# Down weights of 32 experts in two loads of 2 MB, with up-product columns dealt by four

## Chip, cores and metric

The kernel runs on one core of one Trainium2 chip. The metric is the device time of an execution in microseconds. Before the change it is 1321.36 us in the median of three runs (1321.18 to 1321.95).

## What is computed

One inference step of a hybrid decoder layer on 256 prompt tokens and 8 sequences of 8 sample tokens (320 tokens of width 1024), in float32: a modulated norm, an input projection, retention and mLSTM heads, an output projection, then a router that picks 4 of 32 experts for each token, and the final norm. What bears on the change is the experts:

```python
def expert(args):
    xe, e = args
    hu = xe @ w_up[e] + b_up[e]                       # [slots, 1024] @ [1024, 2048]
    gate = jnp.minimum(hu[:, :D_FF], SWIGLU_LIMIT)
    lin = jnp.clip(hu[:, D_FF:], -SWIGLU_LIMIT, SWIGLU_LIMIT)
    glu = gate * jax.nn.sigmoid(SWIGLU_ALPHA * gate)
    return ((lin + 1.0) * glu) @ w_down[e] + b_down[e]  # [slots, 1024] @ [1024, 1024]
```

An expert's up weights are 8 MB, its down weights 4 MB; all 32 experts are loaded, some 400 MB.

## The kernel before, in words

The first 340 us are everything up to the routing. Then comes a loop over the 32 experts. How many tokens an expert gets is known only at run time, and each engine branches (`by_size`, line 290 on) into code for 32, 64, 96 or 128 slots. In this input the experts have, in order, 96, 32, 32, 96, 64, 32, 64, 64, 32, 32, 64, 96, 64, 32, 64, 32, 32, 128, 32, 32, 32, 32, 32, 64, 64, 32, 64, 64, 32, 32, 64 and 64 slots.

Loads. SyncE alone issues them, in order, into six buffers of 16 KB per partition (`SLOT` = 4096 words). The four up pieces (`load_up`, line 432) have 256 rows of `w_up`, two neighbouring rows on a partition, 16 KB, and a buffer each. The four down pieces (`load_down`, line 437) have 256 rows of `w_down`, two neighbouring rows on a partition, 8 KB, in half a buffer each. In one turn of its loop SyncE waits for each of the four up pieces to be used (`piece_done`), then issues the same piece of the next expert, and after that does the same with the down pieces of the expert at hand. A wait holds everything behind it on SyncE. For the last expert the down weights go into buffers 0 and 1 (`load_last`, line 450) in the order 0, 2, 1, 3.

TensorE, per turn (`expert`, line 1105): the up product of expert e (`up`, line 1036, with the bias product in bf16 at line 1040), which waits for each piece; the gather of the next expert's tokens (line 998); the scatter of what expert e-2 gave (line 1094); the transposes of expert e's activations (`turn_activations`, line 1046) and of the weights (line 1102); and the down product of expert e-1 (`down`, bias at 1064, product at 1084). A float32 matmul appears in the trace as two instructions.

Tiling of the up product (`up_products`). With 32 or 96 slots the 128 output columns of the array are cut into four strips of 32, each taking 256 gate and 256 linear columns of the weights, so strip q holds columns 256 q to 256 q + 255 of both. With 64 slots there are two strips of 64, each taking 512 columns; with 128 slots there is one. The strips run at the same time. All moving operands are read with neighbouring elements.

Order of rows in the down product. The contraction runs over the 1024 activation columns, in eight groups of 128. A down piece has rows 256 c + 2 p + h on partition p. So each transpose takes every second column (`h=2` in the rearrangement), and group `piece` meets piece `piece // 2`, row `piece % 2`. In the down product with 32 slots, four strips run side by side, each with its own piece, and each piece is touched in both halves; with 64 slots the pieces 0 and 2 are done at the half; with 96 or 128 they are done one after the other. ScalarE copies the transposed activations out of PSUM (`copy_turned`, line 1476, after all down pieces are used).

Of the kernel before, what the change touches and what calls it, by code (L numbers as in the profile page):

```python
# [13 lines left out]
D = 1024  # L14
KD = D // 128
# [6 lines left out]
NE = 32  # L22
# [7 lines left out]
SLOT = 4096  # L30
# [55 lines left out]
def build(nc, a):  # L86
# [6 lines left out]
    with ctx:  # L93
# [3 lines left out]
        psum = ctx.enter_context(nc.psum_tensor("psum", [128, 8, 512], F32))  # L97

        def at(off, *shape):

            n = int(np.prod(shape))
            assert off + n <= WORDS, (off, shape)
            v = mem[:, off:off + n]
            if len(shape) == 1:
                return v
            names = "abcd"[:len(shape)]
            return v.rearrange(f"p ({' '.join(names)}) -> p {' '.join(names)}",
                               **{k: s for k, s in zip(names, shape)})
# [36 lines left out]
        ident = K("ident")  # L145
# [71 lines left out]
        gt_ = at(o5 + 3072, 2, 512); sg = at(o5 + 4096, 2, 512); li = at(o5 + 5120, 2, 512)  # L217
# [47 lines left out]
        def S(name):  # L265

            if name not in sems:
                sems[name] = ctx.enter_context(nc.semaphore(name))
            return sems[name]

        loaded = [S(f"slot{c}_loaded") for c in range(4)]
        used = [S(f"slot{c}_used") for c in range(4)]
        UP, DOWN = 4, 4
        DOWN_ORDER = (0, 2, 1, 3)
        PIECES = UP + DOWN
        piece_in = [S(f"piece{c}_in") for c in range(PIECES)]
        piece_done = [S(f"piece{c}_done") for c in range(PIECES)]
# [4 lines left out]

        def down_slot(c, *shape):

            return at(4 * SLOT + c * SLOT // 2, *shape)

        def last_slot(c, *shape):

            return at(c * SLOT // 2, *shape)

        def dealt(k):

# [56 lines left out]
        for n in range(4, 16):  # L349
            c = CH[n]  # L350
# [28 lines left out]
        def _(sp):  # L379
# [53 lines left out]

            def load_down(e, c):

                src = a["w_down"][0][e, 256 * c:256 * c + 256, :].rearrange("(p h) n -> p h n", h=2)
                sp.dma_start(down_slot(c, 2, D), src).then_inc(piece_in[UP + c], 16)

            def load_ups(e, it):

# [3 lines left out]

            def load_last(its):

                for i, c in enumerate(DOWN_ORDER):
                    sp.wait_ge(piece_done[i // 2], its)
                    src = a["w_down"][0][NE - 1, 256 * c:256 * c + 256, :].rearrange("(p h) n -> p h n", h=2)
                    sp.dma_start(last_slot(i, 2, D), src).then_inc(S(f"last{c}_in"), 16)  # L450

            def load_downs(e, it):

# [9 lines left out]
            for c in (2, 3, 4, 5, 0, 1):  # L463
                if c < 4:
                    sp.wait_ge(used[c], USES[c])
                elif c == 5:
                    sp.wait_ge(S("y_ready"), len(GROUPS))
                    sp.wait_ge(S("state_out"), 16 * STORES)
                if c < UP:
                    load_up(0, c)  # L470
                else:
                    load_down(0, 2 * c - 8)
                    load_down(0, 2 * c - 7)
            load_ups(1, 1)
            with sp.Fori(2, NE) as e:
                load_ups(e, e)
# [29 lines left out]
        def _(pe):  # L506
# [11 lines left out]
            for k in range(KD):  # L518
                last = pe.transpose(psum[:, 0, 32 * k:32 * k + 9], crow[0:9, 128 * k:128 * k + 128], ident[0:9, 0:9])
# [101 lines left out]
            q = Q["par"]  # L621
            bank_free(q)
            for k in range(KD):
                last = pe.transpose(psum[:, q % BANKS, 32 * k:32 * k + 32], prow[0:32, 128 * k:128 * k + 128],
                                    ident[0:32, 0:32])
            last.then_inc(S("projected"), 1)
            pe.wait_ge(S("params_in"), 16 * 7)
            q = Q["nstate"]
# [8 lines left out]
            for n in range(4, 16):  # L637
# [6 lines left out]
                w = take_chunk(n)  # L644
                if name.startswith("mqk"):

                    for m in range(4):
                        q = Q[f"{name}_{m}"]
                        bank_free(q)
                        for k in range(KD):  # L650
                            if n == 4 and m == 0:
                                pe.wait_ge(S("h_ready"), k + 1)
                            last = pe.matmul(psum[:, q % BANKS, 0:NTOK], w[:, k, 128 * m:128 * m + 128], hT[:, k, :],  # L653
                                             start=(k == 0), stop=(k == KD - 1))
# [32 lines left out]
                if name == "mqk1":  # L687

                    q = Q["gates"]
# [326 lines left out]
            def up_products(slots, weights):  # L1016


                if slots in (32, 96):
                    w = weights.rearrange("p (l n) -> p l n", l=2)  # L1020
                    return [(psum[32 * q:32 * q + 32, g, :], slice(32 * g, 32 * g + 32), w[:, :, 256 * q:256 * q + 256])
                            for g in range(slots // 32) for q in range(4)]
                if slots == 64:
                    return [(psum[64 * q:64 * q + 64, lin, :], slice(0, 64),
                             weights[:, D * lin + 512 * q:D * lin + 512 * q + 512])
                            for lin in range(2) for q in range(2)]
                return [(psum[:, b, :], slice(0, 128), weights[:, 512 * b:512 * b + 512]) for b in range(4)]

            def up(ig, it, slots):

# [12 lines left out]
            def turn_activations(it, slots):  # L1043
                pe.wait_ge(S("act_ready"), it + 1)
                for j in range(KD * slots // 128):
                    last = pe.transpose(flat(4, D)[:, 128 * j:128 * j + 128],  # L1046
                                        gt_.rearrange("p u (w i h) -> p u w h i", w=2, h=2)[:, j // 4, j // 2 % 2, j % 2, :],
                                        ident)
                last.then_inc(S("act_turned"), 1)

            def down(it, slots, meanwhile=None):

                end = meanwhile is not None

                def place(c, *shape):
                    return last_slot(DOWN_ORDER.index(c), *shape) if end else down_slot(c, *shape)

                home = 0 if end else UP
                tiles = 1 if slots == 96 else 128 // slots
                pieces = KD // tiles  # L1060
                pe.wait_ge(S("actT_ready"), it + 2)
                pe.wait_ge(S("bsel_down_ready"), it + 1)
                for u in range(2):
                    pe.matmul(psum[0:slots, 6 + u, :], bsel_down[:, 0:slots],
                              bparts[:, 2 * D + 512 * u:2 * D + 512 * u + 512], start=True, stop=False)
                last = [None] * DOWN
                for j in range(pieces):
                    if end and j == pieces // 2:
                        meanwhile()
                    for u in range(2):  # L1070
                        for q in range(tiles):
                            piece = q * pieces + j
                            c = piece // 2
                            if slots == 96:
                                turned = actT.rearrange("p j s -> p (j s)")[:, 0:8 * slots] \
                                    .rearrange("p (j s) -> p j s", j=KD)[:, piece, :]
                            else:
                                turned = actT[:, j, slots * q:slots * q + slots]
                            if last[c] is None:
                                if end:  # L1080
                                    pe.wait_ge(S(f"last{c}_in"), 16)
                                else:
                                    pe.wait_ge(piece_in[UP + c], 16 * (it + 1))
                            last[c] = pe.matmul(psum[slots * q:slots * q + slots, 6 + u, :], turned,  # L1084
                                                place(c, 2, D)[:, piece % 2, 512 * u:512 * u + 512],
                                                start=(j == 0 and q > 0), stop=(j == pieces - 1))
                for c in range(DOWN):
                    last[c].then_inc(piece_done[home + c], 1)
# [107 lines left out]
        def _(act):  # L1196
# [265 lines left out]
            def copy_turned(it, slots, down_before):  # L1462
                n = 8 * slots
                src = flat(4, n)
                act.wait_ge(S("act_turned"), it + 1)
                if down_before:
                    for c in range(DOWN):
                        act.wait_ge(piece_done[UP + c], it)
                if slots == 96:
                    by_piece = actT.rearrange("p j s -> p (j s)")[:, 0:n] \  # L1470
                        .rearrange("p (q h g s) -> p h g q s", q=4, h=2, g=3)
                    by_turn = src.rearrange("p (g h q s) -> p h g q s", g=3, h=2, q=4)
                    act.copy(by_piece[:, 0], by_turn[:, 0])
                    act.copy(by_piece[:, 1], by_turn[:, 1]).then_inc(S("actT_ready"), 1)
                    return
                act.copy(actT.rearrange("p j s -> p (j s)")[:, 0:n], src).then_inc(S("actT_ready"), 1)  # L1476
# [824 lines left out]
```

## Time and profile before

| what | value |
|---|---|
| median of three runs | 1321.36 us |
| the profiled execution | 1318.82 us, its span 1317.0 us |
| TensorE busy with matmuls | 1173.7 us, 89% of the span |
| mean granted TensorE clock | 0.956 |
| queue of SyncE and ScalarE (q1) | 461.86 MB, 85.2% of 16 engines' span |
| chain that ended last | PE 58%, DMA 35%, DVE 4% |
| loads of up weights | 128 of 2048 KB, 21.8 us from issue to landing in the median |
| loads of down weights | 128 of 1024 KB, 15.8 us |

The span is what the profiler sees from the first to the last instruction. A busy TensorE is not one at its peak, and idle time costs only where an engine is on the chain that ended last. Issue to landing includes the time that a load waits behind earlier ones in the queue.

### The profile page before, as it was taken

What the parts mean: (1) busy time and instruction counts of PE and PEld (TensorE: products, weight loads), DVE (VectorE), ACT (ScalarE), POOL (GpSimd) and SP (SyncE); (2) the same over time, 40 slices, a digit from 0 to 9 for tenths busy, and PEclk for the clock granted to TensorE, in tenths of its full rate; (3) what the DMA queues carried; (4) which work ended last, traced back from release to release, by engine and by line L of the source; (5) the groups of instructions that cost most, each with busy time, mean ns of one, the idle gap of its engine ahead of it and who ended that gap; (6) DMA issues with size and microseconds to landing.
All of it is one profiled execution on the core that took longest, in us unless ns stands there. A gap on an engine that the chain in (4) does not pass through costs nothing.

```text
span 1317.0 us, 23282 instructions
## 1 busy us (share of the span) xinstructions
PE 1173.7 (89%) x8673; PEld 547.2 (42%) x8674; DVE 383.1 (29%) x851; ACT 176.0 (13%) x334; POOL 72.7 (6%) x180
## 2 busy tenths in 40 slices
PE   5999999997879999998899997999877889988886
PEld 4654547444334344443334443444322334333332
DVE  0174215737321221232222221132221221222234
ACT  3012331012111001010101010011001000010001
POOL 1010001323000000000000000000000000000001
PEclk9999999688979999999999998999989999999998
DMA  9935535874469999999999999999999999999992
GB/s 371 364 138 193 212 120 196 242 303 146 183 273 418 404 411 401 426 428 425 428 424 429 419 424 426 426 378 429 427 424 429 423 429 422 425 426 430 424 423 71
DMA packets 62480, 467.34 MB, mean 355 GB/s; under 512 B 6538, under 2 KB 24910, under 8 KB 26730
## 3 DMA queue, kind: packets, MB, share of 16 engines
q1 hardware_dynamic: 59770, 461.86, 85.2%
q10 hardware_dynamic: 2288, 4.37, 1.1%
q0 software_dynamic: 384, 0.59, 0.2%
q8 instruction: 27, 0.44, 0.1%
q14 instruction: 11, 0.09, 0.0%
HBM read 459.78 MB, written 6.42 MB: 354 GB/s over the span
## 4 chain that ended last, share of the span: by engine, by line
PE 58%; DMA 35%; DVE 4%; issue 2%; ACT 1%; POOL 0%; SPq 0%; POOLq 0%; ACTq 0%; DVEq 0%
DMA mem<-in_w_up 33%; PE psum L1036 19%; PE psum L1084 9%; PE psum L672 6%; PE psum L1094 5%; PE psum L653 3%; PE psum L998 2%; PE psum L857 2%; DMA mem<-in_mod_chunks 2%; PE psum L676 2%; PE psum L528 1%; PE psum L803 1%; PE psum L785 1%; PE psum L1046 1%; PE psum L1040 1%
## 5 line engine op out<-in xcount | busy, mean ns | idle before, releaser
L1036 PE MATMUL psum<-mem 128*32 128x512 f32 (+2 forms) x2432 | 396.4, 623 | 83.5 <-DMA mem<-in_w_up 62.2
L1036 PEld LDWEIGHTS psum<-mem 128*32 128x32 f32 (+2 forms) x2432 | 122.1, 123 | 349.4 <-issue 245.9
L1084 PE MATMUL psum<-mem 128*32 128x512 f32 (+3 forms) x1024 | 213.1, 600 | 0.0
L2141 DVE TENSOR_SCALAR mem<-psum 128x256 f32<-128x256 f32 (+3 forms) x32 | 19.2, 601 | 550.2 <-PE psum L1040 550.2
L1094 PE MATMUL psum<-mem 128*128 128x512 f32 x360 | 143.1, 608 | 6.1 <-DVE mem L2142 2.2
L1084 PEld LDWEIGHTS psum<-mem 128*32 128x32 f32 (+3 forms) x1024 | 82.0, 129 | 103.7 <-issue 97.1
L2174 DVE TENSOR_TENSOR mem<-mem,psum 128x1024 f32<-128x1024 f32 (+1 forms) x90 | 94.1, 1045 | 98.6 <-PE psum L1094 98.6
L672 PE MATMUL psum<-mem 128*128 128x512 f32 x192 | 84.2, 595 | 0.0
L998 PEld LDWEIGHTS psum<-mem 128*128 128x128 bf16 x2232 | 74.6, 99 | 19.0 <-issue 18.8
L1459 ACT ACTIVATE mem<-mem 128x256 f32<-128x256 f32 (+3 forms) x32 | 17.9, 561 | 456.9 <-DVE mem L2141 456.9
L998 PE MATMUL psum<-mem 128*128 128x64 bf16 (+1 forms) x2232 | 78.3, 196 | 0.0
L1094 PEld LDWEIGHTS psum<-mem 128*128 128x128 f32 x360 | 49.0, 171 | 54.8 <-issue 52.7
L1666 POOL CAST mem<-mem 128x128 bf16 (+1 forms) x33 | 11.4, 344 | 936.6 <-PE psum L1084 902.6
L672 PEld LDWEIGHTS psum<-mem 128*128 128x128 f32 x192 | 36.0, 190 | 43.7 <-issue 43.6
L2112 DVE TENSOR_SCALAR mem<-mem 128x128 bf16<-128x128 f32 (+1 forms) x99 | 22.2, 281 | 65.4 <-issue 65.3
L1476 ACT COPY mem<-psum 128x256 f32<-128x256 f32 (+2 forms) x29 | 14.0, 484 | 184.2 <-PE psum L1084 184.2
L653 PE MATMUL psum<-mem 128*128 128x320 f32 x128 | 36.6, 447 | 2.0 <-DVE mem L1726 2.0
L1216 ACT COPY mem<-psum 128x320 f32<-128x320 f32 (+9 forms) x65 | 25.0, 395 | 94.9 <-PE psum L672 68.1
L1482 ACT COPY mem<-psum 128x320 f32<-128x320 f32 x32 | 13.7, 429 | 157.5 <-PE psum L1094 150.6
L857 PE MATMUL psum<-mem 128*128 128x512 f32 x64 | 31.9, 657 | 1.2 <-ACT mem L1379 1.2
L528 PE MATMUL psum<-mem 128*32 128x128 f32 x768 | 24.8, 284 | 7.9 <-DMA mem<-in_mod_chunks 6.9
L1493 ACT COPY mem<-psum 128x1024 f32<-128x1024 f32 x31 | 31.6, 1018 | 0.0
(275 smaller groups left out, 815.3 us busy)
## 6 DMA issues: line engine op xcount, KB each, us to landing
mem<-in_w_up SPq DMA_DIRECT2D x128, 2048.0 KB, 21.8
mem<-in_w_down SPq DMA_DIRECT2D x128, 1024.0 KB, 15.8
mem<-in_mod_chunks SPq DMA_DIRECT2D x12, 2048.0 KB, 12.1
mem<-in_in_chunks SPq DMA_DIRECT2D x8, 2048.0 KB, 9.8
mem<-in_out_chunks SPq DMA_DIRECT2D x2, 2048.0 KB, 10.3
mem<-in_x_prompt ACTq DMA_DIRECT2D x2, 1024.0 KB, 6.2
mem<-in_state_ret SPq DMA_DIRECT2D x4, 512.0 KB, 8.6
mem<-in_state_mlstm_c SPq DMA_DIRECT2D x4, 512.0 KB, 7.7
```

Of the source, the lines that this page charges most:

```text
L528: last = pe.matmul(psum[32 * t:32 * t + 32, bank, 0:128], cT[:, k, :], w[:, k, 128 * t:128 * t + 128], start=(k == 0), stop=False)
L653: last = pe.matmul(psum[:, q % BANKS, 0:NTOK], w[:, k, 128 * m:128 * m + 128], hT[:, k, :], start=(k == 0), stop=(k == KD - 1))
L672: last = pe.matmul(psum[:, q % BANKS, :], hT[:, k, tok(t)], w[:, k, :], start=(k == 0), stop=(k == KD - 1))
L676: last = pe.matmul(psum[64 * u:64 * u + 64, q % BANKS, 0:256], hT[:, k, tok(t)], w[:, k, 256 * u:256 * u + 256], start=(k == 0), stop=(k = ...
L857: last = pe.matmul(psum[:, 6 + u, :], hT[:, k, tok(t)], w[:, k, :], start=(k == 0), stop=(k == KD - 1))
L998: last = pe.matmul(psum[:, 4 + k // 4, 128 * (k % 4):128 * (k % 4) + slots], h2p[:, part, t, dealt(k)], P[:, t, 0:slots], start=(part == 0 ...
L1036: last = pe.matmul(out, xg[:, 2 * c + h, cols], moving, start=(c + h == 0), stop=False)
L1084: last[c] = pe.matmul(psum[slots * q:slots * q + slots, 6 + u, :], turned, place(c, 2, D)[:, piece % 2, 512 * u:512 * u + 512], start=(j = ...
L1094: last = pe.matmul(out, G[:, tok(t)], yd[:, u, :], start=True, stop=True)
L1216: act.copy(*pairs[-1]).then_inc(S("evacuated"), 1)
L1493: act.copy(yd.rearrange("p u n -> p (u n)"), flat(6, D)).then_inc(S("y_copied"), 1)
L2174: TT(v, v, src, ALU.add).then_inc(S("added"), 1)
```

## The change

Down weights come in two pieces of 2 MB, 512 rows each, four neighbouring rows (16 KB) on a partition, and the number of down pieces and of their semaphores is two instead of four. Row 512 c + 4 p + h lies on partition p of piece c. To match, the up products deal the columns: the moving operand is read with a step of four elements, so that strip q of four holds columns 4 i + q, strip q of two the columns 4 i + 2 q + h, and with 128 slots a bank holds its 512 columns as four runs of every fourth column. The transposes then read neighbouring columns. The same holds for the bias rows in bf16. The down product takes piece j // (pieces // 2) at step j for all strips together. The last expert's pieces go in the order 0, 1. ScalarE's copy for 96 slots has a new order.

```diff
-        UP, DOWN = 4, 4
-        DOWN_ORDER = (0, 2, 1, 3)
+        UP, DOWN = 4, 2
...
-            return at(4 * SLOT + c * SLOT // 2, *shape)
+            return at(4 * SLOT + c * SLOT, *shape)
...
-            return at(c * SLOT // 2, *shape)
+            return at(c * SLOT, *shape)
...
-                src = a["w_down"][0][e, 256 * c:256 * c + 256, :].rearrange("(p h) n -> p h n", h=2)
-                sp.dma_start(down_slot(c, 2, D), src).then_inc(piece_in[UP + c], 16)
+                src = a["w_down"][0][e, 512 * c:512 * c + 512, :].rearrange("(p h) n -> p h n", h=4)
+                sp.dma_start(down_slot(c, 4, D), src).then_inc(piece_in[UP + c], 16)
...
-                for i, c in enumerate(DOWN_ORDER):
-                    sp.wait_ge(piece_done[i // 2], its)
-                    src = a["w_down"][0][NE - 1, 256 * c:256 * c + 256, :].rearrange("(p h) n -> p h n", h=2)
-                    sp.dma_start(last_slot(i, 2, D), src).then_inc(S(f"last{c}_in"), 16)
+                for c in range(DOWN):
+                    sp.wait_ge(piece_done[c], its)
+                    src = a["w_down"][0][NE - 1, 512 * c:512 * c + 512, :].rearrange("(p h) n -> p h n", h=4)
+                    sp.dma_start(last_slot(c, 4, D), src).then_inc(S(f"last{c}_in"), 16)
...
-                    load_down(0, 2 * c - 8)
-                    load_down(0, 2 * c - 7)
+                    load_down(0, c - 4)
...
                 if slots in (32, 96):
-                    w = weights.rearrange("p (l n) -> p l n", l=2)
-                    return [(psum[32 * q:32 * q + 32, g, :], slice(32 * g, 32 * g + 32), w[:, :, 256 * q:256 * q + 256])
+                    w = weights.rearrange("p (l c i q) -> p q l c i", l=2, c=2, q=4)
+                    return [(psum[32 * q:32 * q + 32, g, :], slice(32 * g, 32 * g + 32), w[:, q])
                             for g in range(slots // 32) for q in range(4)]
                 if slots == 64:
-                    return [(psum[64 * q:64 * q + 64, lin, :], slice(0, 64),
-                             weights[:, D * lin + 512 * q:D * lin + 512 * q + 512])
+                    w = weights.rearrange("p (l c i q h) -> p l q c h i", l=2, c=2, q=2, h=2)
+                    return [(psum[64 * q:64 * q + 64, lin, :], slice(0, 64), w[:, lin, q])
                             for lin in range(2) for q in range(2)]
-                return [(psum[:, b, :], slice(0, 128), weights[:, 512 * b:512 * b + 512]) for b in range(4)]
+                w = weights.rearrange("p (b i h) -> p b h i", b=4, h=4)
+                return [(psum[:, b, :], slice(0, 128), w[:, b]) for b in range(4)]
...
-                                        gt_.rearrange("p u (w i h) -> p u w h i", w=2, h=2)[:, j // 4, j // 2 % 2, j % 2, :],
-                                        ident)
+                                        gt_.rearrange("p u n -> p (u n)")[:, 128 * j:128 * j + 128], ident)
...
-                            piece = q * pieces + j
-                            c = piece // 2
+                            c, h = j // (pieces // 2), q * (pieces // 2) + j % (pieces // 2)
...
-                                                place(c, 2, D)[:, piece % 2, 512 * u:512 * u + 512],
+                                                place(c, 4, D)[:, h, 512 * u:512 * u + 512],
...
-                        .rearrange("p (q h g s) -> p h g q s", q=4, h=2, g=3)
-                    by_turn = src.rearrange("p (g h q s) -> p h g q s", g=3, h=2, q=4)
+                        .rearrange("p (c q g s) -> p c g q s", c=2, q=4, g=3)
+                    by_turn = src.rearrange("p (g c q s) -> p c g q s", g=3, c=2, q=4)
```

## Rows read from the trace of the kernel before

**Rows 1.** The page, what the DMA engines moved in each of 40 slices

```profile
GB/s 371 364 138 193 212 120 196 242 303 146 183 273 418 404 411 401 426 428 425 428 424 429 419 424 426 426 378 429 427 424 429 423 429 422 425 426 430 424 423 71
```

**Rows 2.** The page, DMA issues: line, count, KB each, us to landing

```profile
mem<-in_w_up SPq DMA_DIRECT2D x128, 2048.0 KB, 21.8
mem<-in_w_down SPq DMA_DIRECT2D x128, 1024.0 KB, 15.8
```

**Rows 3.** The chain that ended last, in order of time: start us, us, what

```profile
561.86 21.77 DMA mem<-in_w_up
...
585.79 27.35 DMA mem<-in_w_up
...
615.31 27.36 DMA mem<-in_w_up
...
820.06 3.47 PE psum L1036 x16
...
838.39 27.73 PE psum L1036 x64
...
1240.36 25.65 DMA mem<-in_w_up
```

**Rows 4.** Windows: busy by engine, then granted clock, DMA share, GB/s

```profile
1009.50:1028.90 19.40, 17.06 (x93) 5.50 (x91) 3.63 (x9) 1.77 (x3) 0.57 (x2) 1.00 1.01 430
1029.10:1038.80 9.70, 8.81 (x98) 4.70 (x99) 3.17 (x5) 1.23 (x2) 0.00 (x0) 1.00 1.02 424
...
459.20:461.70 2.50, 1.33 (x15) 0.16 (x3) 1.61 (x6) 0.93 (x3) 0.53 (x2) 1.00 0.24 52
...
491.50:503.00 11.50, 11.50 (x64) 3.79 (x66) 0.00 (x0) 1.50 (x2) 0.00 (x0) 1.00 0.98 367
...
878.00:881.00 3.00, 2.02 (x20) 0.42 (x13) 1.52 (x6) 1.01 (x2) 0.55 (x2) 1.00 0.10 11
```

**Rows 5.** Timeline of SyncE: start us, us from first to last issue, count

```profile
488.14 10.63 SPq L437 DMA_DIRECT2D mem<-in_w_down  x4
...
724.83 10.63 SPq L437 DMA_DIRECT2D mem<-in_w_down  x4
...
879.87 2.06 SPq L437 DMA_DIRECT2D mem<-in_w_down  x4
...
1220.98 1.89 SPq L437 DMA_DIRECT2D mem<-in_w_down  x4
```

**Rows 6.** Timeline of TensorE: start us, us, line, shape, count, idle before

```profile
447.46 0.84 PE L1040 MATMUL psum<-mem 128*32 128x512 bf16 x12
...
484.38 13.89 PE L1084 MATMUL psum<-mem 128*96 128x512 f32 x32
...
642.72 3.65 PE L1036 MATMUL psum<-mem 128*64 128x512 f32 x16 [1.24 <-DMA mem<-in_w_up]
...
661.53 20.81 PE L1036 MATMUL psum<-mem 128*32 128x512 f32 x192 [1.11 <-issue]
...
876.11 3.60 PE L1084 MATMUL psum<-mem 128*32 128x512 f32 x29
...
909.88 7.08 PE L1036 MATMUL psum<-mem 128*32 128x512 f32 x64
...
929.87 3.64 PE L1036 MATMUL psum<-mem 128*32 128x512 f32 x32 [0.98 <-issue]
...
1287.08 0.38 PE L1064 MATMUL psum<-mem 128*64 128x512 bf16 x1 [1.83 <-ACT mem L1493]
```

**Rows 7.** Up loads issued 340 to 360 us, then down loads 480 to 510

```profile
DMA to landing us min/median/max: 7.7/8.7/10.0
```

```profile
DMA to landing us min/median/max: 6.3/6.6/7.1
```

**Rows 8.** Groups by line and form: weight loads of the two kinds of transposes

```profile
L1046 PEld LDWEIGHTS psum<-mem 128*128 128x128 f32 x106 | 17.8, 202 | 18.8 <-issue 18.8
...
L1102 PEld LDWEIGHTS psum<-mem 128*128 128x128 f32 x66 | 8.6, 147 | 1.2 <-issue 1.2
```

More of the change, by code:

```diff
@@ L1055, in place @@
                 def place(c, *shape):
-                    return last_slot(DOWN_ORDER.index(c), *shape) if end else down_slot(c, *shape)
+                    return last_slot(c, *shape) if end else down_slot(c, *shape)
                 home = 0 if end else UP
@@ L1071, in down @@
                         for q in range(tiles):
-                            piece = q * pieces + j
-                            c = piece // 2
+                            c, h = j // (pieces // 2), q * (pieces // 2) + j % (pieces // 2)
                             if slots == 96:
                                 turned = actT.rearrange("p j s -> p (j s)")[:, 0:8 * slots] \
-                                    .rearrange("p (j s) -> p j s", j=KD)[:, piece, :]
+                                    .rearrange("p (j s) -> p j s", j=KD)[:, j, :]
                             else:
```

## The prediction, made before the changed kernel was run

> **What bounds the kernel now.** Read first the page's 40 slices and its DMA issues [rows 1, 2]. From slice 13 on (slices of 32.9 us, so from some 395 us) the DMA engines move 378 to 430 GB/s without a break, more than anywhere before: this is the loop over the 32 experts, in which 128 loads of 2 MB (up) and 128 of 1 MB (down) are waited for. The chain in order of time [rows 3] then says which of the two, queue or TensorE, sets the end at each point. It is TensorE until 561.86 us, DMA from there to 820.06, TensorE again through the one expert with 128 slots (27.73 us at 838.39), then DMA again; its last step, 25.65 us from 1240.36, ends at 1266, and a tail of 51 us on the arithmetic of the last expert follows. So the end moves with the instant at which the last up piece lands, and that instant depends on (1) the rate of the queue, (2) the moments at which it runs dry, (3) TensorE where it is on the chain.
>
> For (1) the windows [rows 4] hold stretches of one kind: up pieces alone run at 430 GB/s, down pieces alone at 424. For (2) the same view shows it dry twice (a DMA share of 0.24 and 0.10) and ill fed once (367 GB/s at 491.5 to 503). The SyncE timeline [rows 5] shows why: the next down loads are issued only as the matmuls of the down product before them end. For (3) see TensorE's timeline [rows 6].
>
> **The change, part by part.** The profiled execution took 1318.82 us (span 1317.0); the median of the runs is 1321.36. I make the sum as a difference and put it on the median. About 0.2%, 2.6 us, is what a measurement of this kernel can tell from no change.
>
> *Larger runs.* A partition's share of a down load becomes 16 KB from 8 KB, as for the up weights; no row shows down weights so loaded, but the up rows have the same run and size. 4.19 MB at 424 GB/s take 9.89 us and at 430 take 9.75 us: 0.14 us less for each expert's four megabytes [rows 4]. Bounds: nothing, or 0.2 us if the windows' edges hide some. Two DMA issues fewer per expert save nothing, SyncE waits on others anyway [rows 5].
>
> *Freeing the buffers.* Four counters become two. With 32 slots the old order touches all four pieces in the first half of the product and frees none before the end; the new one frees the first 2 MB halfway, half of 3.60 us [rows 6] or 1.8 us earlier. That matters only where the queue is dry: at 461 and at 880 [rows 4]. Elsewhere a down load waits behind 10 us or more of transfers (issue to landing is 15.8 us in the median [rows 2]) and nothing comes of it. With 64 slots half was free at the half before as well, though only 1 MB could be issued, as the second piece in order was freed at the end: no difference where the queue is long. With 96 or 128 slots the old kernel frees 1 MB each 3.43 us (issues 488.14 to 498.44, four of them), the new one 2 MB at the second and at the fourth of these moments. There are three such products with 96 slots and one with 128; the last comes behind a full queue, and for the first TensorE has no need of the data for a long time. Two count, at 484 and 721 [rows 6].
>
> - At 484: the first 2 MB go out at 491.57 instead of 1 MB at 488.14. The queue is dry by then (the old one was just short of it: 367 GB/s). On an empty queue 2 MB need at least 7.7 us from issue to landing [rows 7], so they land at 499.3; the second 2 MB, issued at 498.44, at 506.1. Before, the last 1 MB issued at the same time landed 6.3 to 7.1 us later, 504.7 to 505.5 [rows 7]. Everything behind it is later by 0.6 to 1.4, and more if the queue fills slowly again; I take **+1.5**. The moment is set by TensorE, so what was won at 461 is lost here.
> - Four groups of down loads at -0.14 follow until TensorE waits for up pieces at 642.72 [rows 6]: +1.5 - 0.6 = +0.9, passed on to TensorE. It runs without a wait for DMA from there through up at 661.53 (20.81 us) to the down product at 721.
> - At 721: the fourth issue was at 735.1 (724.83 + 10.63 less the 0.3 of the issue itself [rows 5]); the second 2 MB are issued at 735.1 + 0.9 = 736.0 and land 7.7 later, 743.7, against 735.1 + 6.3 = 741.4 before, by the same rows as above. Shift **+2.3**. Two more groups until 820: +2.0.
> - TensorE takes that through the 128-slot expert to the down product at 876.11. Its first piece comes free at 879.87 + 2.0 - 1.8 = 880.1, against 879.87 [rows 5]. The queue was dry from about 878 to 881 before; now it starts again 0.2 to 0.8 later, say **+0.5**.
> - From there to the last up piece there are 13 groups of down loads (issues 879.87 to 1220.98 [rows 5]): 13 x 0.14 = **-1.8**. The 128-slot down at 896 falls behind a queue 10 us long, its cover.
>
> Sum: -1.3. In the tail the last down product begins at 1287.08 behind a wait for ScalarE, not for a load [rows 6], so two pieces for four change nothing.
>
> *Transposes* read adjacent columns instead of every second one: 106 weight loads of 202 ns (L1046) against 147 for those of L1102, which are already adjacent [rows 8]. Most of it hides beside the matmuls and behind DMA; on the chain before 461 there are 16 (six, two, two and six for the first four experts), at most 0.9 us. As the down product at 484 moves with them I add -0.1, nearer nothing than the full difference.
>
> *Up products* now read their moving operand with a step of four elements, 16 bytes. Column count, passes and results are unchanged, so nothing can be won here. No row shows such a read. The nearest is the bf16 bias product of L1040: twelve matmuls of 512 columns in 0.84 us in four column strips at a time [rows 6], so four streams together pass 6144 elements in at most 0.84 us (7.3 per ns). The strided f32 up product asks for 64 x 512 elements in 7.08 us, 4.6 per ns. If only elements count, cost zero; if each element needs a fetch of its own, up to the fourfold time of the four-strip forms (28 us for 7.08, what 128 slots take). I take zero, since the demand in elements is the smaller, and price the other end as a rival.
>
> The Trainium skill speaks against this part: "SBUF — State Buffer", section "Door 1: The DMA port swizzle", says SBUF has lines of 16 bytes, that a line must be hit twice for the access to be hidden, and that the free step ends at four fp32; "Advanced Engine Details and Errata", section "SBUF Cachelines", says a different line for each access is penalised. A step of exactly four fp32 stands on that edge. The trace of before has no row that shows it either way; by the strict reading the sum would be the first rival's.
>
> Total: -1.3 - 0.1 = -1.4: **1320.0 us** (1317.4 for the profiled execution).
>
> **Rivals.** *A, slower: the strided moving operand.* Place: L1036 with 32 or 96 slots (four strips), then 64 (two). It decides as soon as the up product outlasts its cover. With 32 slots the cover is 9.5 us: such an expert takes TensorE 20.0 us (909.88 to 929.87 [rows 6]) of the queue's period of 29.5 (585.79 to 615.31 [rows 3]). So doubling 7.08 costs nothing while DMA is ahead. The three 96-slot products have none: 20.81 more each, 62; two 32-slot ones stand on TensorE's chain before 461 (the experts after the first), 14 more; of 76 the queue's lead takes back a few: about +70, **1391 us**. If the strips lose only a third, 1/3 of 62 and of 14 is 25, less the same lead: 1340 or below. If two strips are hit too, the 64-slot experts, whose period is full, bring it over 1450. For it: no row shows this read free. Against: four bf16 streams already pass more elements.
>
> *B, faster: the refills after 96 slots cost nothing.* The old queue was underfed there too; if 2 MB recover at once, the +1.5 and the rest of +2.3 fall away. Then the shift is -0.6 at 642, -0.9 at 820, -0.9 - 1.8 = -2.7 at 880 and -1.8 more at the end: -4.5, **1316.9 us**. Against it: on an empty queue 7.7 us are the least that 2 MB took [rows 7].
>
> *C, runs no faster:* if the rate goes by something else than the run's length (the place of the buffer, the 4 KB rows), the terms of 0.14 vanish: 19 x 0.14 = 2.7 back, **1322.7 us**.
>
> **How the numbers follow.** Forecast 0.45, A 0.30, B 0.17, C 0.08. Of the forecast 0.38 is within 0.2%, 0.04 above it on the fast side, 0.03 on the slow. Faster: 0.04 + 0.15 of B = 0.19. Same: 0.38 + 0.02 + 0.06 = 0.46. Slower: 0.30 + 0.03 + 0.02 = 0.35. Low end 1316 just takes in B. The upper end takes in the third-cost form of A, 1340, which leaves out the rest of A, some 0.18. Without A the forecast's own range is 1317 to 1323.
>
> **What would show it.** Right: windows of down loads alone at 430 GB/s; up groups x64 still 7.08 and x192 still 20.81 at full clock; the gap at 461 nearly gone; a drier stretch at 491 to 504 and one at 735; the up wait at 642.7 about 0.9 later; the last up piece landing 1.4 earlier. Wrong: L1036 groups longer at clock 1.0 (A); share near 1 through 491 to 504 (B); down windows still at 424 (C).

## The result and the profile after

The changed kernel takes 1643.52 us in the median of four runs (1642.12 to 1645.03), against 1321.27 for the kernel before in the same comparison: a ratio of 1.246, 95% interval 1.243 to 1.249. The profiled execution took 1642.39 us (span 1640.6), 323.6 us more than the span of before. The forecast was 1320.0 us, the range ended at 1340.

The page of the changed kernel, parts 1, 2 and 4, says where to look:

```profile
PE 1557.3 (95%) x8672; PEld 577.9 (35%) x8674; DVE 382.4 (23%) x851; ACT 176.0 (11%) x334; POOL 72.4 (4%) x180
...
PEclk9999996998999999999999999999999999999998
...
GB/s 374 285 146 224 94 283 265 164 104 200 369 251 260 232 381 296 279 423 360 223 221 238 376 292 427 243 151 366 421 429 429 324 279 387 287 299 423 340 205 47
...
PE 92%; DVE 3%; issue 2%; DMA 2%; ACT 1%; POOL 0%; SPq 0%; POOLq 0%; ACTq 0%; DVEq 0%
PE psum L1035 47%; PE psum L1081 12%; PE psum L1091 9%; PE psum L670 5%; PE psum L996 4%; PE psum L651 2%; PE psum L855 2%; PE psum L1039 1%; PE psum L674 1%; DMA mem<-in_in_chunks 1%; PE psum L526 1%; PE psum L1099 1%; DMA mem<-in_mod_chunks 1%; PE psum L1045 1%; PE psum L801 1%
```

DMA has gone from 35% of the chain to 2%, and the queue that ran near 425 GB/s through most of the expert loop [rows 1] is now under 400 GB/s in all but six slices of it. Nearly half of the chain is one line, the up product (1036 before, 1035 now). The granted clock is at full speed in nearly all slices, as before (mean 0.978, before 0.956), so a lower clock is not the reason. TensorE's timeline shows the up products of each kind, one expert each with 96, 64, 32 and 128 slots, and bias products behind two of them (start us, us, line, shape, count):

```profile
458.94 43.62 PE L1035 MATMUL psum<-mem 128*32 128x512 f32 x192 [1.15 <-issue]
...
502.35 1.58 PE L1039 MATMUL psum<-mem 128*32 128x512 bf16 x12
...
517.15 29.05 PE L1035 MATMUL psum<-mem 128*64 128x512 f32 x64 [1.12 <-issue]
...
687.38 14.59 PE L1035 MATMUL psum<-mem 128*32 128x512 f32 x64
...
1034.89 57.84 PE L1035 MATMUL psum<-mem 128*128 128x512 f32 x64 [1.30 <-issue]
...
1092.56 2.00 PE L1039 MATMUL psum<-mem 128*128 128x512 bf16 x4
```

Against [rows 6] the 96-slot product went from 20.81 to 43.62 us, the 32-slot one from 7.08 to 14.59, and against [rows 3] the one with 128 slots from 27.73 to 57.84. The one with 64 slots took 13.95 us before, where now it takes 29.05:

```profile
461.66 13.95 PE L1036 MATMUL psum<-mem 128*64 128x512 f32 x64 [1.17 <-issue]
```

The factor is 2.06 to 2.10 in each, whether four strips run side by side, two, or one alone. The bf16 bias products of 96 slots went from 0.84 to 1.58. In the groups by line, all up products together:

```profile
L1035 PE MATMUL psum<-mem 128*32 128x512 f32 (+2 forms) x2432 | 773.7, 1082 | 25.7 <-issue 25.7
...
L1039 PE MATMUL psum<-mem 128*32 128x512 bf16 (+2 forms) x152 | 32.5, 635 | 0.0
```

Before, the page had 396.4 us busy with 83.5 us of idle time before them, 62.2 of it waiting for up weights, and the bias products 19.7 us. So 377 + 13 us of work came in and 58 us of waiting went: 332 us, of which the span shows 324. No wait of an up product for its weights is left. The other direction of the change, the loads, is hidden behind this and had to be measured apart.

### The profile page after: what moved, and what is told of

Read it like the earlier page. It is cut to its first block, busy times and chain, and to the rows that moved or that the text cites. A ratio compares the mean times of both kernels' runs of the same rounds, so it can differ in the third digit from the quotient of the medians.

```text
span 1640.6 us, 23064 instructions
## 1 busy us (share of the span) xinstructions
PE 1557.3 (95%) x8672; PEld 577.9 (35%) x8674; DVE 382.4 (23%) x851; ACT 176.0 (11%) x334; POOL 72.4 (4%) x180
## 4 chain that ended last, share of the span: by engine, by line
PE 92%; DVE 3%; issue 2%; DMA 2%; ACT 1%; POOL 0%; SPq 0%; POOLq 0%; ACTq 0%; DVEq 0%
PE psum L1035 47%; PE psum L1081 12%; PE psum L1091 9%; PE psum L670 5%; PE psum L996 4%; PE psum L651 2%; PE psum L855 2%; PE psum L1039 1%; PE psum L674 1%; DMA mem<-in_in_chunks 1%; PE psum L526 1%; PE psum L1099 1%; DMA mem<-in_mod_chunks 1%; PE psum L1045 1%; PE psum L801 1%
## 5 line engine op out<-in xcount | busy, mean ns | idle before, releaser
L1035 PE MATMUL psum<-mem 128*32 128x512 f32 (+2 forms) x2432 | 773.7, 1082 | 25.7 <-issue 25.7
L1035 PEld LDWEIGHTS psum<-mem 128*32 128x32 f32 (+2 forms) x2432 | 158.4, 138 | 606.2 <-issue 605.6
L1039 PE MATMUL psum<-mem 128*32 128x512 bf16 (+2 forms) x152 | 32.5, 635 | 0.0
```

Source lines behind the costliest of these rows:

```text
L1035: last = pe.matmul(out, xg[:, 2 * c + h, cols], moving, start=(c + h == 0), stop=False)
L1039: last = pe.matmul(out, bsel[:, cols], moving, start=False, stop=True)
```

## The experiments

In what follows the moving operand is the third argument of `pe.matmul` (here rows of weights), the stationary one the second; the trace shows the loading of the stationary operand as LDWEIGHTS on PEld.

The working theory after the result, S: the step of four elements in the moving operand of the up products is the whole loss. Its rivals: L, the loads take part in it; and for the nature of the cost, T1 (distance), T2 (two hits in one place hide the access), T3 (short runs or more dimensions of the pattern).

**1. The step alone, in the kernel before.**

```diff
-                    w = weights.rearrange("p (l n) -> p l n", l=2)
-                    return [(psum[32 * q:32 * q + 32, g, :], slice(32 * g, 32 * g + 32), w[:, :, 256 * q:256 * q + 256])
+                    w = weights.rearrange("p (l c i q) -> p q l c i", l=2, c=2, q=4)
+                    return [(psum[32 * q:32 * q + 32, g, :], slice(32 * g, 32 * g + 32), w[:, q])
```

and in the same way for 64 and 128 slots, as in the change.

> The kernel before with nothing but the new moving operands of the up products (f32 and bias rows), loads and all else as before; activation columns come out in another order, so the sums are not the reference's. Theory S (the step of 16 bytes in the moving operand is the whole loss): up products of 32 slots about 14.7 us and of 96 about 43.6 as in the changed kernel, time 1640 +- 6. Rival L (the loads of 2 MB or the later release take part in it): clearly below 1635, with the rest left to the loads.

It took 1645.69 us in one run. From its timeline:

```profile
463.43 43.67 PE L1037 MATMUL psum<-mem 128*32 128x512 f32 x192 [1.11 <-issue]
...
573.92 14.59 PE L1037 MATMUL psum<-mem 128*32 128x512 f32 x64
```

The step of four elements, with the old loads, makes the whole loss: the changed kernel took 1643.52. L falls.

**2. The loads alone.** The changed kernel with the six lines of `up_products` as they were.

```diff
-                    w = weights.rearrange("p (l c i q) -> p q l c i", l=2, c=2, q=4)
-                    return [(psum[32 * q:32 * q + 32, g, :], slice(32 * g, 32 * g + 32), w[:, q])
+                    w = weights.rearrange("p (l n) -> p l n", l=2)
+                    return [(psum[32 * q:32 * q + 32, g, :], slice(32 * g, 32 * g + 32), w[:, :, 256 * q:256 * q + 256])
```

> The changed kernel with the moving operands read as before, neighbouring elements; down loads of 2 MB and transposes as changed; the activation columns meet the wrong rows of the down weights, so the sums are not the reference's. Theory S: up products back at 7.1, 13.95, 20.8 and 27.7 us, and by the rest of the prediction 1320.0 us (1317 to 1323), down loads at 430 GB/s, last up load landed about 1.3 us earlier, dry stretch after 491. Rival L: 1330 or more. Rival B of the prediction: 1317 or less.

1313.74 us in the median against 1319.05 for the kernel before on that chip; ratio 0.9969, interval 0.9952 to 0.9986: 1.8 to 6.3 us faster. The windows (up loads alone, then down loads alone) and SyncE's timeline show the steps of the prediction:

```profile
1005.80:1025.20 19.40, 16.04 (x87) 4.69 (x87) 2.95 (x8) 1.77 (x3) 0.53 (x2) 1.00 1.01 429
1025.40:1035.00 9.60, 8.31 (x97) 4.51 (x98) 2.68 (x4) 1.23 (x2) 0.00 (x0) 1.00 1.01 428
...
459.00:461.50 2.50, 1.38 (x7) 0.50 (x8) 0.56 (x3) 1.78 (x3) 0.00 (x0) 1.00 1.01 380
...
490.00:504.00 14.00, 14.00 (x85) 4.39 (x84) 0.00 (x0) 1.50 (x2) 0.53 (x2) 1.00 0.84 311
```

```profile
490.13 7.20 SPq L436 DMA_DIRECT2D mem<-in_w_down  x2
...
876.72 2.05 SPq L436 DMA_DIRECT2D mem<-in_w_down  x2
```

Down loads now move at the rate of up loads (428 against 424 before [rows 4]); the gap at 461 is closed (share 1.01 for 0.24); and the stretch after the 96-slot product is dry as forecast (share 0.84 over 14 us), since 2 MB go out only at 490.13 and again some 6.9 us later.

**3. Pairs of neighbours.** The loads of the change, and a layout that deals two neighbouring columns at a time: strip q holds the columns 512 (q // 2) + 4 i + 2 (q % 2) + h. The transposes take every second column again.

```diff
+                    w = weights.rearrange("p (l c i v h) -> p c v l i h", l=2, c=2, v=2, h=2)
+                    return [(psum[32 * q:32 * q + 32, g, :], slice(32 * g, 32 * g + 32), w[:, q // 2, q % 2])
...
+                            if tiles == 4:
+                                c, h = q // 2, 2 * (q % 2) + j
```

> The changed kernel with its loads of 2 MB and four neighbouring rows, but the up products deal pairs of neighbouring columns: two elements next to each other, then a jump to the next 16 bytes (bias rows: next 8 bytes). Transposes read every second column as before. Computes the reference. Theory T1 (what costs is that the next element is not the neighbour, by its distance): half of the steps are 4 bytes and half 12, so half of the extra cost stays, about 10.9 us for a 32-slot up product, and 1380 to 1500. Theory T2 (two hits on the same 16 bytes hide the access): 7.1 us, and a time like the kernel with the loads alone, 1320, perhaps 1 us more since the 32-slot down product frees nothing at its half. Theory T3 (short inner runs or more dimensions cost): 14 us or more, 1640.

1326.44 us, ratio 1.0063 (1.0044 to 1.0083). Its up products:

```profile
406.56 7.52 PE L1035 MATMUL psum<-mem 128*32 128x512 f32 x64
428.81 21.98 PE L1035 MATMUL psum<-mem 128*32 128x512 f32 x192 [1.11 <-issue]
```

Only 5.6% over 20.81. T1 asked for half of the extra cost, T3 for all of it; both fall. T2 stands, except that pairs are not quite free. The time is above the 1320 expected. Beside run 2 this kernel starts the expert loop 2.3 us later, and the first awaited up load after the 128-slot expert lands 12.3 us later (950.67 against 938.33); the last one still lands 12.2 later. So what it loses, it loses where TensorE is on the chain. The 5% are there, but so is the release at the half of the 32-slot down products, which run 2 has and this kernel lacks; how the loss divides between the two was not measured.

**4. Runs of 128, three dimensions.**

```diff
-                    w = weights.rearrange("p (l n) -> p l n", l=2)
+                    w = weights.rearrange("p (l c q i) -> p q l c i", l=2, c=2, q=4)
...
-                return [(psum[:, b, :], slice(0, 128), weights[:, 512 * b:512 * b + 512]) for b in range(4)]
+                w = weights.rearrange("p (c b i) -> p b c i", b=4, c=4)
+                return [(psum[:, b, :], slice(0, 128), w[:, b]) for b in range(4)]
```

> The kernel before, the moving operands cut into runs of 128 neighbouring elements from different places (three dimensions), so the sums are not the reference's. T1 and T2: nothing changes, 1319 to 1323. T3 (dimensions or jumps cost): above 1330.

1322.2 us in one run, and the 96-slot product takes 20.81 us as before:

```profile
430.73 20.81 PE L1037 MATMUL psum<-mem 128*32 128x512 f32 x192 [1.12 <-issue]
```

Jumps between runs of 128 elements and a third dimension cost nothing by themselves.

**5 to 8. Which step costs, in elements or in bytes.** In the kernel before, one step at a time. Step 2, the form for 32 and 96 slots:

```diff
+                    w = weights.rearrange("p (l c i h) -> p c h l i", l=2, c=2, h=2)
+                    return [(psum[32 * q:32 * q + 32, g, :], slice(32 * g, 32 * g + 32), w[:, q // 2, q % 2])
```

Step 3, the same form:

```diff
-                    return [(psum[32 * q:32 * q + 32, g, :], slice(32 * g, 32 * g + 32), w[:, :, 256 * q:256 * q + 256])
+                    return [(psum[32 * q:32 * q + 32, g, :], slice(32 * g, 32 * g + 32), w[:, :, 64 * q:64 * q + 768:3])
```

Step 8, over both rows of a buffer, in the f32 products alone:

```diff
+                if weights.dtype == F32:
+                    def eighth(k):
+                        return weights[:, k:k + 4089:8]
```

And the step of four of the change in the bf16 bias products alone:

```diff
+                strided = weights.dtype == BF
+                if strided:
```

> The kernel before, the moving operands of the up products with a step of two elements: 8 bytes in f32, 4 bytes in the bf16 bias rows; columns in another order, so the sums are not the reference's. Theory B (bytes decide, 16 for two new elements' worth; f32 at 8 bytes is still two hits on 16): up products as before, 7.1 us for 32 slots, 1320. Theory E (any step beyond the neighbour costs, in elements): 14.7 us and 1640. Theory G (a step of 8 bytes costs as it did for the bf16 rows, whose 12 products went from 0.84 to 1.6 us at 8 bytes): f32 14.7 us, the bias rows unchanged at 0.84.

> The same with a step of three elements, 12 bytes in f32 and 6 in bf16; not the reference's sums. Theory B: between, every fourth 16 bytes is hit once only: 7.1 to 9 us for 32 slots. Theory E and G: 14.7 us, 1640. If the bias rows stay at 0.84 us the bound for bf16 lies above 6 bytes.

> The same with a step of eight elements, 32 bytes, in the f32 operands alone, the bias rows as before; not the reference's sums. If the cost is one fixed price per element that is not beside the one before: 14.6 us for 32 slots as with a step of four, 1630. If it grows with the distance: above 20 us, 1900 or more.

> The kernel before with the step of four elements (8 bytes) in the bf16 bias rows alone; not the reference's sums. Bias products of a 96-slot expert 0.84 to 1.6 us, those of a 32-slot one 0.39 to 0.7; TensorE is on the chain for a third of the experts, so 1320 to 1327. All theories agree on the time; the twelve products decide whether 8 bytes cost without the f32 operands around them.

They took 1325.28, 1458.31, 1649.66 and 1319.3 us, one run each, beside 1316.64 for one run of the kernel before. The 96-slot up product and its twelve bias products, step 2:

```profile
427.64 21.93 PE L1037 MATMUL psum<-mem 128*32 128x512 f32 x192 [1.12 <-issue]
449.36 0.90 PE L1041 MATMUL psum<-mem 128*32 128x512 bf16 x12
```

Step 3:

```profile
445.87 32.78 PE L1035 MATMUL psum<-mem 128*32 128x512 f32 x192 [1.16 <-issue]
478.42 1.26 PE L1039 MATMUL psum<-mem 128*32 128x512 bf16 x12
```

Step 8, f32:

```profile
462.99 44.34 PE L1046 MATMUL psum<-mem 128*32 128x512 f32 x192 [1.11 <-issue]
```

Step 4, bf16 alone:

```profile
428.08 20.81 PE L1048 MATMUL psum<-mem 128*32 128x512 f32 x192 [1.11 <-issue]
448.70 1.54 PE L1052 MATMUL psum<-mem 128*32 128x512 bf16 x12
```

| step, elements | 96-slot up product, f32, us | factor | twelve bias products, bf16, us |
|---|---|---|---|
| 1 | 20.81 | 1 | 0.84 |
| 2 | 21.93 | 1.05 | 0.90 |
| 3 | 32.78 | 1.58 | 1.26 |
| 4 | 43.62 | 2.10 | 1.54 |
| 8 | 44.34 | 2.13 | not run |

In f32 the cost rises to a step of four and stays nearly the same at eight, the longest step tried. Counted in aligned groups of four elements, a step of two needs half a group per element, a step of three three quarters, a step of four or more a whole one: 2.10 times these is 1.05, 1.58 and 2.10, which is what f32 took. (For neighbours the same count would give 0.53; the measured 1 says that something else sets the pace there.) Theory B came nearest for f32 but was too kind at step 3, where a 32-slot product took 11.02 us and not 7 to 9. E and G fall with step 2. In bf16 the same steps in elements cost 1.07, 1.50 and 1.83 times as much, nearly as in f32, although they are half as long in bytes.

**9. Two loads of 2 MB without longer runs.** Each load has two runs of 8 KB per partition; columns and transposes as before.

```diff
+                src = a["w_down"][0][e].rearrange("(v w p h) n -> w p v h n", v=2, w=2, h=2)[c]
+                sp.dma_start(down_slot(c, 2, 2, D), src).then_inc(piece_in[UP + c], 16)
```

> Two down loads of 2 MB, each of two runs of 8 KB per partition, and everything read as before: computes the reference. No longer runs, and with 32 slots no release at the half. What the loads alone gained (ratio 0.997) came from the runs (13 groups at 0.14 us after 880) and from the release at the half: here both are missing and the refills after 96 slots stay, so 1 to 4 us slower than the kernel before, and down windows at 424 GB/s. If larger transfers as such were the gain: 1313 to 1317.

1319.17 us against 1316.55, ratio 1.0015 (0.9997 to 1.0034). Larger transfers as such bring nothing that is measured. What run 2 gained came with what this one lacks, the runs of 16 KB and the order in which they free the buffers. The traces show the first of the two apart. From some 940 us to the end of the loop nearly every expert waits for up weights; eleven periods lie between the first and the last awaited up load of that stretch. In this run:

```profile
918.12 24.53 DMA mem<-in_w_up
...
1241.83 25.66 DMA mem<-in_w_up
```

In run 2:

```profile
915.71 22.62 DMA mem<-in_w_up
...
1236.08 25.52 DMA mem<-in_w_up
```

Start and length added give a period of 29.53 us for an expert here and of 29.39 in run 2. The kernel before has 29.52 (from 941.24 to 1266.01). Runs 3 and 12, which have the runs of 16 KB but no release at the half with 32 slots, have 29.38 and 29.36. So runs of 16 KB are worth 0.14 us or little more for each expert, which is what the prediction gave them, and the order of release has no part in it.

**10. The same step on the stationary side.**

```diff
-                                        gt_.rearrange("p u (w i h) -> p u w h i", w=2, h=2)[:, j // 4, j // 2 % 2, j % 2, :],
+                                        gt_.rearrange("p u (i h) -> p u h i", h=4)[:, j // 4, j % 4, :],
```

> The kernel before with the transposes of the activations (their stationary operand) read with a step of four elements in place of two; for 32 and 96 slots partly over other columns, not the reference's sums. If a step of four costs the stationary operand as it cost the moving one: weight loads of L1046 up from 0.2 to 0.3 us and more, eight transposes 1.1 to about 1.7 us, the time 1 to 4 us longer. If the stationary side is free: no change.

1316.32 us in one run. The groups by form have the weight loads of the transposes:

```profile
L1046 PEld LDWEIGHTS psum<-mem 128*128 128x128 f32 x106 | 17.5, 202 | 19.2 <-issue 19.2
```

202 ns, as with a step of two [rows 8]. Eight transposes take 1.12 us, 1.11 before. So a step of four elements in the stationary operand costs no more than a step of two. That is not the same as free: in run 2, where the transposes read adjacent columns, the same loads take 140 ns and eight transposes 1.03 us.

```profile
L1044 PEld LDWEIGHTS psum<-mem 128*128 128x128 f32 x106 | 13.3, 140 | 20.5 <-issue 20.5
```

**11. Pairs inside and astride a group of four.** f32 alone, pairs eight elements apart: elements 2 and 3 of each eight for 64 slots, 3 and 4 for 32 and 96.

```diff
+                    eights = weights.rearrange("p (i f) -> p i f", f=8)
+                    if slots in (32, 96):
+                        return [(psum[32 * q:32 * q + 32, g, :], slice(32 * g, 32 * g + 32), eights[:, :, 3:5])
...
+                    if slots == 64:
+                        return [(psum[64 * q:64 * q + 64, lin, :], slice(0, 64), eights[:, :, 2:4])
```

> The kernel before, f32 moving operands read as pairs of neighbours with a jump of eight elements between pairs: for 64 slots the pairs lie inside an aligned group of four elements (2, 3), for 32 and 96 slots astride two groups (3, 4). Not the reference's sums. Theory F (an aligned group of four elements must be hit twice in a row): 64 slots about 14.6 us as with a step of two, 32 slots 14.7 and 96 slots 43.6 us. Theory N (a neighbour next hides the jump, wherever it lies): 7.45 and 21.95 us for 32 and 96 too. Time 1400 by F, 1325 by N.

1430.0 us in one run, 30 above the 1400 expected by F. One product of 96 and one of 64 slots:

```profile
457.21 43.63 PE L1044 MATMUL psum<-mem 128*32 128x512 f32 x192 [1.11 <-issue]
...
610.31 14.88 PE L1044 MATMUL psum<-mem 128*64 128x512 f32 x64 [1.12 <-issue]
```

Two neighbours astride a boundary of four elements cost as much as no neighbours at all, 43.63 us; two inside one cost 14.88 us, where the run with step 2 has 14.62. The two cases were run with different numbers of slots; that this is not the reason is seen from a step of four, which costs the same factor in both. Theory F holds, N falls.

**12. Hybrid.** The loads of the change; neighbours as the moving operand for 64 and 128 slots with every fourth column in the transposes, pairs for 32 and 96.

```diff
+                    if slots in (32, 96):
+                        taken = gt_.rearrange("p u (w i h) -> p u w h i", w=2, h=2)[:, j // 4, j // 2 % 2, j % 2, :]
+                    else:
+                        taken = gt_.rearrange("p u (i h) -> p u h i", h=4)[:, j // 4, j % 4, :]
```

> The changed kernel's loads; up products with 64 and 128 slots read neighbours and their transposes take every fourth column, with 32 and 96 slots pairs of neighbours and every second column. Computes the reference. If the stationary step of four is free: 14 us for 64 slots in place of 14.6 with pairs, so 3 to 6 us less than pairs everywhere, 1319 to 1323, no better than the kernel before because the 96-slot products still take 21.98 for 20.81 and nothing is freed at the half. If the stationary step costs: 1325 or more.

1319.66 us against 1316.55, ratio 1.0026 (1.0011 to 1.0041). Moving the step to the stationary operand for 64 and 128 slots took back a part of what pairs everywhere lost (ratio 1.0063 in run 3, though against the kernel before on another chip), but it does not beat the kernel before: a 96-slot product takes 22.05 us for 20.81. No arrangement that was tried gives 32 and 96 slots both contiguous moving operands and four neighbouring rows on a partition.

## Why the prediction was wrong, and where it was right

*The step that failed* is the one on the up products, "I take zero, since the demand in elements is the smaller". It compared the elements per ns of four strips together, taken from the bf16 bias products, with what the strided f32 product asks for. That row was read with neighbouring elements, four to each group of four. It bounded elements, and by the experiments the cost goes by groups. Runs 1, 3, 5 to 7 and 11 show in its place: a moving operand that takes one element from each aligned group of four (f32) needs 2.1 times as long, one that takes two 1.05 to 1.07 times. The term put at zero measured 377 us of up products and 13 us of bias products, less 58 us of waits that they filled.

*Rival A* named the place and the sign, with a chance of 0.30, but not the price. It had the cost begin with the number of strips side by side, and the product of 128 slots free of it. The trace shows the same factor for four strips, two and one (2.10, 2.08, 2.09). So the 64-slot experts, whose period was full, and the 128-slot one pay too, and the form of A that was priced, 1391, leaves them out. The prediction had that case in one clause ("over 1450") and outside its range.

The price could have been worked out from rows: with a factor of 2.1 the 64-slot product takes 29.3 us, and with scatter, gather and down product TensorE's turn is some 43 us where the queue's is 29.5; twelve such experts alone bring over 150 us. A also held most of the 32-slot experts to be covered by the queue. They were not. By form the up products grew by 178 us with 64 slots, by 169 us with 32 and 96 together, of which three 96-slot products are 68, and by 30 us with 128. No up product waits for its weights any longer: the queue, now under 400 GB/s in most slices, is ahead of TensorE.

*The rule that was cited against the change* deserved more weight. In f32 the runs show two elements of an aligned group at 1.05 to 1.07, one at 2.10, and a pair astride two groups at 2.10 too. The Trainium skill, "SBUF — State Buffer", section "Door 1: The DMA port swizzle", asks for two hits on the same 16 bytes; with that rule the f32 runs agree. The bf16 runs do not: a step of four hits the same 16 bytes twice, and takes 1.54 us for 0.84. Its next clause, that four fp32 or eight bf16 can be stepped for free, does not hold for the moving operand here either: four fp32 cost 2.10 times, and four bf16 are already at 1.83.

*A reading that was too short.* The prediction has DMA on the chain from 561.86 to 820.06. The chain has matmuls in the middle of that, from 642.72 to 771 us; its own bullets on the loads use the right stretch, so the sum does not suffer.

*The terms of the loads*, by run 2. TensorE starts the expert loop 1.6 us earlier there than before (338.03 against 339.60). In the traces of this case that instant lies between 337.5 and 343.5 us, with the same TensorE code ahead of it, so shifts are counted from that start.

- Rate: 428 and 432 GB/s in two windows of down loads, where 430 was expected, and 0.14 us for each expert (run 9). Rival C falls.
- Gap at 461: closed, as forecast, and lost again at 491, as forecast. Rival B falls.
- After 491: as forecast, the first 2 MB go out at the moment of the old second load (490.13 here; 488.14 + 3.43 = 491.57 before, less 1.6 for the start). The share of 0.84 over 14 us is 2.2 us of idle queue. The up wait that was at 642.72 comes at 641.85, 0.7 later when the start is taken off; forecast was +0.9. The one at 820.06 comes at 820.19, 1.7 later; forecast was +2.0.
- At the end of the loop: the last step of the chain that is DMA (run 9 shows the line) ends at 1261.60, before at 1266.01.

That is 4.4 earlier, 2.8 when the start is taken off. In run 2 the last up piece before the 128-slot expert took 1.93 us where it took 3.47 before [rows 3], at a granted clock of 1.00 against 0.54. No run ties these 1.5 us to the change: with the old loads the same piece took 3.64 us in run 10 and 1.92 in run 8. What is left, 1.3, is the forecast's 1.3 for the loads, and the steps on the way are within 0.3 us of it. But the measured ratio, 1.8 to 6.3 us, lies wholly beyond it, and the profiles are one execution of each: how much more the loads gain, and where, stays open.

*Transposes*: reading adjacent columns took their weight loads from 202 to 140 ns, as the 147 of L1102 suggested, and almost none of it reaches the chain. Six transposes take 0.82 us where they took 0.87, so sixteen of them save 0.13 us, and the term of -0.1 has the right size.

## What to carry to other kernels

Before dealing columns for the sake of a load, look at which operand pays: a step of four elements doubled the time of the f32 up products, which read it in their moving operand, in all three tilings, while in the stationary operand of a transpose it cost no more than a step of two, and hardly any time of TensorE beside adjacent columns. When no row shows an access pattern, a rate in elements from a contiguous row is no bound for it, and the price of the bad case belongs in the sum over all experts whose period is full, not only in the ones already on the chain. A gain of 1.4 us does not pay for an unknown on 400 us of matmuls: measure the unknown alone first.

## What the runs showed that was not expected

- The factor does not depend on the strips. In f32, four strips with a step of four pass one element each in 1.77 ns (43.62 us for 192 x 512 / 4 = 24576 elements of a strip), one strip alone the same (57.84 us for 64 x 512 = 32768).
- In f32 the cost stops growing: 2.10 at a step of four and 2.13 at eight.
- In bf16 the cost rises with the step in elements as in f32, and so at half of the bytes: 1.26 us at 6 bytes and 1.54 at 8, for 0.84. Whether it stops growing at four elements, and whether aligned groups of 8 bytes are the reason, was not tried.
- In the stationary operand steps of two and of four cost the same, 202 ns for a weight load, and adjacent columns 140: there the count of groups does not describe the cost.
